# Three moves in the written-out order of a one-core hybrid mixer kernel: the gated output, the projection pieces, and one weight split

## The reference, cut to what matters

```python
h = rms_norm(x, g_pre) * (1 + scale) + shift
(sg_u, sg_v, sg_gate, dq, dk, dv, d_gate, nq, nk, nv, n_gate, f_gate, merge) = split(h @ w_in)
y_sg   = u * (W_s @ rms_norm(v) + b)                                  # spatial gating
y_diff = rms_norm((softmax(q1 k1) - lam * softmax(q2 k2)) @ v, subln) # differential attention, 4 heads
y_na   = neighbourhood_attention(nq, nk, nv, context, bias)           # 8 heads
y_f    = real(fft2(h))                                                # Fourier mixing
mixed  = sum_b sigmoid(merge_b) * ((y_b * silu(gate_b)) @ p_b)        # four branches
x      = x + gate * rms_norm(mixed @ w_out, g_post)
```

## Time and profile before

| | |
|---|---|
| Median of 3 runs | 1981.79 us (1981.74 to 1983.77) |
| The profiled execution, its own time | 1982.85 us |
| Its span in the profile | 1980.9 us |
| TensorE matmul busy | 1903.0 us, 96% of the span |
| VectorE busy | 960.9 us, 49% |
| ScalarE busy | 678.3 us, 34% |
| GpSimd busy | 593.8 us, 30% |
| Mean granted TensorE clock | 0.989 |

### The profile page before, as it was taken

One profiled execution on the slowest core, in us unless ns is written; L12 is line 12 of the kernel. 1 busy time (PEld: TensorE's weight loads), 2 busy tenths in 40 slices (PEclk: granted clock), 3 DMA queues, 4 the chain that ended last, 5 costly groups with the idle time before them and its releaser, 6 DMA issues.

```text
span 1980.9 us, 31159 instructions
## 1 busy us (share of the span) xinstructions
PE 1903.0 (96%) x12512; PEld 1762.9 (89%) x12512; DVE 960.9 (49%) x1536; ACT 678.3 (34%) x1293; POOL 593.8 (30%) x278
## 2 busy tenths in 40 slices
PE   6799999999999999999999999999999999999997
PEld 3697888989999999999878988988999999999996
DVE  5799788634355462421352144666244546433123
ACT  4322355424433221321352234453334332222221
POOL 2434322222222332233334332222322223323331
PEclk8999999999999999999999999999999999999999
DMA  8444421121111211122332221111212112212231
GB/s 305 145 164 140 164 97 43 54 83 67 65 65 65 94 66 54 65 75 75 128 117 75 91 75 65 49 49 43 96 65 75 54 65 95 75 35 83 75 126 55
DMA packets 50958, 172.16 MB, mean 87 GB/s; under 512 B 6656, under 2 KB 7296, under 8 KB 50816
## 3 DMA queue, kind: packets, MB, share of 16 engines
q1 hardware_dynamic: 41024, 146.60, 21.3%
q10 hardware_dynamic: 9792, 23.58, 3.3%
HBM read 162.82 MB, written 7.34 MB: 86 GB/s over the span
## 4 chain that ended last, share of the span: by engine, by line
PE 80%; DVE 12%; issue 3%; ACT 3%; DMA 1%; POOL 0%; SPq 0%; ACTq 0%; DVEq 0%; POOLq 0%
PE ps L1661 56%; PE ps L1549 4%; PE ps L1551 4%; PE ps L1550 4%; DVE mixed L1089 3%; PE ps L1768 2%; PE ps L1777 1%; PE ps L1787 1%; PE ps L1727 1%; PE ps L1742 1%; DMA stage<-in_w_mod 1%; DVE nparts L1313 1%; ACT Pm L998 1%; DVE Pm L1375 1%; PE ps L1812 1%
## 5 line engine op out<-in xcount | busy, mean ns | idle before, releaser
L733 POOL TENSOR_TENSOR wlo<-raw,whi 128x1024 fp32r<-128x1024 f32 x224 | 563.4, 2515 | 1233.0 <-ACT whi L791 1230.6
L1661 PE MATMUL ps<-bufB,whi 128*128 128x320 f32 x2816 | 539.4, 314 | 7.1 <-DVE vn L1215 3.9
L1661 PE MATMUL ps<-bufA,whi 128*128 128x320 f32 x2816 | 537.3, 313 | 5.3 <-DVE z L1495 1.4
L1661 PEld LDWEIGHTS ps<-bufB,whi 128*128 128x128 f32 x2816 | 441.4, 189 | 16.9 <-issue 12.3
L1661 PEld LDWEIGHTS ps<-bufA,whi 128*128 128x128 f32 x2816 | 439.3, 188 | 15.0 <-issue 10.4
L1661 PE MATMUL ps<-bufB,wlo 128*128 128x320 f32 x1408 | 322.0, 310 | 0.0
L1661 PE MATMUL ps<-bufA,wlo 128*128 128x320 f32 x1408 | 321.4, 309 | 0.0
L791 ACT ACTIVATE whi<-raw 128x1024 fp32r<-128x1024 f32 x224 | 237.5, 1060 | 212.3 <-PE ps L1661 123.6
L1661 PEld LDWEIGHTS ps<-bufB,wlo 128*128 128x128 f32 x1408 | 236.3, 189 | 0.0
L1661 PEld LDWEIGHTS ps<-bufA,wlo 128*128 128x128 f32 x1408 | 235.7, 188 | 0.0
L1495 DVE SCALAR_TENSOR_TENSOR z<-gate_m,ps 128x640 f32<-128x640 f32 x48 | 39.4, 821 | 226.2 <-PE ps L1661 225.6
(11 more groups left out here) (230 smaller groups left out, 2043.1 us busy)
## 6 DMA issues: line engine op xcount, KB each, us to landing
raw<-in_wstream SPq DMA_DIRECT2D x224, 512.0 KB, 3.2
stage<-in_wstream SPq DMA_DIRECT2D x32, 512.0 KB, 4.2
stage<-in_w_mod SPq DMA_DIRECT2D x16, 512.0 KB, 15.2
out_y_sample<-X ACTq DMA_DIRECT2D x8, 512.0 KB, 2.7
Pm<-in_rpb ACTq DMA_DIRECT2D x12, 256.0 KB, 2.9
X<-in_x_sample SPq DMA_DIRECT2D x4, 512.0 KB, 10.9
xres<-in_x_sample ACTq DMA_DIRECT2D x4, 512.0 KB, 5.1
xres<-out_y_sample ACTq DMA_DIRECT2D x4, 512.0 KB, 5.2
```

The lines of the kernel that those rows point to most:

```text
L733: pool.tensor_tensor(wlo[:, s % SPLITS, :], raw[:, s % RAWS, :], whi[:, s % SPLITS, :].bitcast(F32), ALU.subtract).then_inc(sems["lo"], 1)
L1661: ins = pe.matmul(ps[:, 2 * b + n, 0:HALF], wt[:, cols], src[:, part, base + k, n * HALF:(n + 1) * HALF], start=k == 0 and wt is hi and pa ...
```

## The change

Three moves in the order; no operation is added, removed or resized.

1. In `differential()`, `YT` of a finished head stood at the end of the segment of the next head's t = 4 unit, behind its `CB` and in front of the next scores (units 9, 14 and 19). It now stands right behind the scores step `S` of that unit. The last head's `YT` stays.
2. `interleave` gets more places. In `differential()` one before the first scores, and one before each of `TP` and `PV` of the last unit: 46 places for 64 pieces in place of 43. In `neighbourhood()` one before the first unit: 43 places for 103 pieces in place of 42.
3. In `Plan.__init__`, the one slot of layer 1 that would be split at the step `T sgv 3, 0` is split at the last `VN` instead, so behind the squares of all five tiles.

```diff
@@ def differential():
-    out, late, norm = [], [], []
+    out, norm = [None], []
     for u, (f, hh, t) in enumerate(units):
         out += [("S", "diff", u, f, hh, t, 0)] + norm + [None]
         norm = []
@@
-        out += [("CB", "diff", u, f, hh, t)] + late
-        late = []
-        if f and t < 3:
-            norm = [("NR", "diff", f - 1, t)]
-        if f and t == 3:
-            late = [("YT", "diff", f - 1)]
+        out.append(("CB", "diff", u, f, hh, t))
+        if f and t < 4:
+            norm = [("NR", "diff", f - 1, t) if t < 3 else ("YT", "diff", f - 1)]
     u = len(units) - 1
-    out += [("TP", "diff", u, *units[u]), ("PV", "diff", u, *units[u])] + late
+    out += [None, ("TP", "diff", u, *units[u]), None, ("PV", "diff", u, *units[u])]
@@ def neighbourhood():
-    out, late = [], []
+    out, late = [None], []
@@ class Plan: def __init__(self):
             if self.layer[self.first_of_slot[n]] and self.steps[self.first_of_slot[n]] == ("T", "sgv", 3, 0):
                 floor = self.at[1, ("T", "sgv", 0, 2)]
+            if self.layer[self.first_of_slot[n]] and i == self.at[1, ("T", "sgv", 3, 0)]:
+                i = self.at[1, ("VN", TILES - 1)]
             self.issue.setdefault(max(i, floor), []).append(n)
```

## The result

| | before | after |
|---|---|---|
| Median of 5 runs each | 1982.1 us (1981.74 to 1983.77) | 1991.71 us (1988.4 to 1993.44) |
| The profiled execution, its own time | 1982.85 us | 1990.2 us |
| Its span | 1980.9 us | 1988.3 us |
| Mean granted TensorE clock | 0.989 | 0.988 |

The ratio is 1.0045, with a 95% interval of 1.0035 to 1.0056: slower by 9.6 us in the medians and by 7.4 in the two profiled executions, where 1964 and a gain were forecast.

A forecast was written before the change was run, and what follows sets the result against it. TensorE, 96% busy, was taken as the bound: its work plus idle gaps and low-clock stretches. The terms summed to -17.9 us, from the profiled 1982.85 to 1964.95, or 1964 us as a median; eight-in-ten range 1956 to 1974.

The forecast's parts named there:

- Where the gates' ends fall: Differential attention: moving gates' tanh and multiply saves 3.6 us, a new wait at unit 3's transposes costs 3.5; net -0.1.
- the last unit: End of differential attention: pieces fill the gaps around transposes and `PV`, a new wait precedes the last `YT`; -8.4 us, both layers.
- neighbourhood attention: Two pieces cover the 0.5 us keys' wait before the first scores, -1.0; +1.0 allowed for pieces dealt anew; sum 0.0.
- what `YT` stands ahead of: Layer 0 around units 7 and 9, VectorE full: `YT` ahead of transposes and combination makes TensorE wait 4.4 for 2.7; +1.7 us.
- one piece ahead elsewhere: Other transposes with one piece ahead: one GpSimd subtraction per layer lengthens a VectorE operation and shows as a wait; +2.6 us.
- the price of a piece: Twelve matmuls take 1.76 us and two pieces about 3.7, so one piece covers 1.85 us of waiting.
- The squares: Layer 1: splitting last cuts TensorE's 3.85 us idle to about 0.25 and removes the half clock, -3.6 and -2.9; together -6.5 us.
- Rival (a): Squares don't gain: something else holds `VN`, the gap stays above 2.5 us and the clock falls; 1969 us, chance 0.08.
- A piece before the first scores: Differential attention, both layers: a piece fills the 0.9 us wait for VectorE's last copy of V; -1.8 us.
- Scores behind a short unit: Differential attention: waits for L998 at units 6 and 11 vanish, unit 16's falls to about 0.55; -5.4 us over both layers.
- Rival (d): Slower: GpSimd's subtractions block VectorE at most of the 24 transposes with one piece ahead; 1992 us, chance 0.05.
- Rival (b): Last unit's gap moves to `YT 3`: a longer GpSimd hold makes the 1.1 into 3 and drops the clock; 1971 us, chance 0.12.

The follow-up runs named there:

- the place in neighbourhood attention with the gates' pieces later: Kernel before with only the extra neighbourhood-attention place, and the first pieces of `F ngate 0` and `F ngate 1` one place later: 1985.92 us, ratio 1.002.
- the later split: Changed kernel with the weight split at the first piece of `F dgate 3` issued one piece later, pieces unmoved: 1981.55 us, ratio 1.0001 to the kernel before.
- the last three single edits: Squares' and `YT`'s moves plus one edit each: `YT` behind the pieces ahead, 1978.53 us; piece before first scores, 1964.24; last unit's pieces moved, 1968.65.
- best version: Squares' and `YT`'s moves, the head piece, and a piece before the last transposes taken from ahead in unit 19: 1961.67 us, ratio 0.9892 to the kernel before.
- head piece: Kernel with squares' and `YT`'s moves, plus one piece before the first differential scores, taken from ahead in unit 3: 1964.24 us, ratio 0.9911 to the kernel before.

## Why the prediction was wrong

The sum was missed by 25 us in the profiles, and five terms carry it. With both layers together, waits and clock read from the rows of before and after, "Where the gates' ends fall" was put at -0.1 and came to about +8; the last unit at -8.4 and came to about 0; neighbourhood attention at 0.0 and came to +6.4; what `YT` stands ahead of at +1.7 and came to about +6; one piece ahead elsewhere at +2.6 and came to +3.7. The other terms came out near their figures. (Read this way the terms overlap by some 1.5 us, where TensorE waits at the low clock.)

**What bounds the kernel, the price of a piece:** right, as far as it went, but for "the other stages have almost no wait": before, TensorE waits 3.36 us at 1020.52 for VectorE at the start of layer 1, and idles 29 us in the 181 before the first query transposes. No move touches these. What was missing is said below: a wait has two prices, its length and whether the clock falls behind it.

**The squares, -6.5:** right. -6.7 from the last `H` transposes to the first query transposes, -6.5 in the medians of that part alone; no wait for `vn`, the clock at 1.00. Rival (a) fell. Of the 6.5, 2.9 were clock, and that size is partly luck: with the squares as before, the wait of 3.8 to 3.9 us cost 3.4 us of clock in the profiles of three kernels (before, the places alone, and the place in neighbourhood attention with the gates' pieces later) and 1.7 in those of two (`YT` alone, and the place in neighbourhood attention alone).

**A piece before the first scores, -1.8:** right. From the first query transposes to the first scores the changed kernel takes 0.8 us longer in each layer with one piece of 1.85 more, so 1.05 less, 2.1 in both layers.

**Where the gates' ends fall, -0.1:** the step that failed first. The old waits went but for 0.3 in layer 0, and a new one did come where it was put, but at 3.8 us and not 1.5, and with the clock down. The forecast priced the gate there (1.7, by the later split) and left GpSimd to a separate term, one hit per layer, worth 1.3, at a random place. The trace has three per layer on the way to transposes, at units 3, 5 and 18. At unit 3 there was no slack, so the hit of 2.1 us counted in full, and the clock behind it (1.7 a layer) was priced nowhere. Here it isn't random: what delays VectorE, the end of a projection, is the neighbour in the list of what starts GpSimd, the beginning of the next. The rule of the Trainium skill that the prediction named (SBUF — State Buffer, "Who interferes with whom") has the trace on its side: an add of 128x2 took 2.24 us under a subtraction and 0.16 without.

**Scores behind a short unit, -5.4:** the waits went nearly as forecast, -4.6: unit 12 has a new one of 0.4 in each layer. But `YT`'s move alone takes most of them, which the text didn't separate.

**What YT now stands ahead of, +1.7 in layer 0:** right in kind. `YT 0` waits 2.4 us for VectorE's scaling, and the clock is low until 324, 1.4 + 2.0 us lost from 316 on. The walk through the queues had 1.1 before the context's scores of unit 7 (2.0 came), 1.8 before the transposes in unit 9 and 1.5 before its `PV` (none came), and none for `YT` itself; and it priced no clock.

**One piece ahead elsewhere, +2.6:** the waits at units 5 and 18, 1.0 and 0.8 in each layer, are 3.7 in all. The size of a hit was right (2.15 forecast; 2.2 and 1.6 here), and so was the slack of 0.8 at unit 18; at unit 5, where 2.6 stood, it was 1.2. The number of hits was wrong, two per layer here beside the one at unit 3. Rival (d) asked for them at most of the 24 transposes; they came at 6. That its time, 1992, is the measured one is chance. (Its "18 of the 24 have 2.6 us of slack" should read 16: of the twelve in a layer, eight have two pieces behind in the unit before.)

**The last unit, -8.4:** wrong. No wait at its transposes or `PV`, and 1.5 and 0.2 in front of and behind the last `YT`, where 1.1 and 0.2 were forecast: that much held. But "the buffers differ" looked at one pair of projections only. `YT 2` takes one buffer, so in the new order `M 0 6` and `M 0 7` both have the other, and they now meet in one place: 2.2 us for the tanh that stands behind `YT 2`'s copy and the exponentials, and the clock falls behind it in layer 1.

```profile
1365.12 0.74 ACT L797 ACTIVATE bufA<-z 128x640 fp32r<-128x640 f32 x1 [5.41 <-DVE z L1418]
...
1367.53 0.70 ACT L1032 ACTIVATE gate_m<-ps 128x640 f32<-128x640 f32 x1
1368.37 1.28 PE L1660 MATMUL ps<-bufB,whi 128*128 128x320 f32 x4 [2.17 <-ACT gate_m L1032]
```

The kernel with the places alone bears this out: its `YT 2` stands later, so `M 0 6` and `M 0 7` have different buffers, and there is no wait between them and no fall of the clock in the last unit. It takes both moves together to make this wait. Rival (b) had the 1.1 grow to 3 by GpSimd; it stayed at 1.5, and was not the cause.

**Neighbourhood attention, 0.0:** wrong, +6.4 in the stages and +6.5 by the part alone. The -1.0 wasn't there because the piece needs the buffer that is being copied; the +1.0 for the new deal had no reading behind it, and the new deal puts a projection's begin right behind `VT`.

**What would show it.** Of the signs named, the waits for `vn`, of the first scores and of `PV` for L1019 went, the one at unit 4 and the one before the last `YT` came (3.8 and 1.4 to 1.5, for 1.5 and 1), and layer 0 waits longer around unit 9. Of the signs of being wrong one came: the mean clock didn't rise from 0.989, it went to 0.988.

**The bounds and the chances.** Each part's bounds held only for itself. The forecast gave 0.05 to slower, by one mechanism that had to be everywhere. It was enough that pieces moved at all: the deal changed in 13 of 20 units and in most of neighbourhood attention, and each projection has a begin, which wants a buffer and starts a split, and an end, which wants ScalarE and VectorE. The ones that cost most: the split behind `F dgate 2`, `M 0 7` behind `M 0 6`, and the begins behind `VT`. The falls of the clock added about 6.8 us in differential attention.

What stays open: 1.3 us of layer 1's neighbourhood attention; the exact size of the split's test; and when a wait brings a fall of the clock and how long that lasts. The last is part of the spread between runs of one kernel, 5 us for the changed one: of the 15 runs of the kernel before that ran beside the last three single edits, the slowest, 1984.44 us, has the lowest mean clock, 0.986, and the fastest, 1979.85, the highest, 0.991.

## What to carry to other kernels

Filling a wait with a piece of other work moves every piece behind it. List for both orders where each projection begins (whose buffer it takes, by what stands before it in the list, and which split it starts) and ends (what it puts in front of ScalarE and VectorE) before counting the wait that is covered; here the one piece that was worth it, about -4 us, left all pieces from unit 4 on where they were. Measure the parts alone: of four, two gained 14 us together and two lost 15. And price a wait twice, for its length and for the clock behind it, the second as a range: `YT 0`'s 2.4 us brought 1.7 or 3.4 us, the 2.2 us in the last unit nothing or 1.7.

## What the runs showed of the hardware

What the clock took in an attention stage, summed over its windows, was 1.7 us before in each layer; 6.9 and 3.4 in the changed kernel; 5.2 and 0 with `YT` alone; 1.7 and 0 in the best version. How much a wait brings isn't set by its length:

| wait of TensorE | us | clock behind it, us |
|---|---|---|
| unit 3's transposes | 3.8 | 1.7 in all four places (changed kernel and places alone, both layers) |
| for `vn`, squares | 3.8 to 3.9 | 3.4 in three kernels, 1.7 in two |
| `YT 0`, layer 0 | 2.4 | 3.4 in four kernels, 1.7 in three (split later, head piece, best version) |
| for `gate_m`, last unit of the changed kernel | 2.2 | 0 in layer 0, 1.7 in layer 1 |
| unit 3's transposes, split later | 1.7 | 0 in both layers |
| last unit before, 0.8 and 1.7 within 2 us | 2.5 | 1.7 in both layers; with the place in neighbourhood attention alone, 1.7 and 5.1 |
| last unit, `YT` alone, 1.4 and 0.4 | 1.8 | 1.7 in layer 0, 0 in layer 1 |

The smallest VectorE operations lost as much time to GpSimd as a large one. Under a GpSimd subtraction of 128x1024, an add of 128x2 took 2.24 us for 0.16, an operation of 128x1 took 2.40 for 0.22, and each ended with the subtraction; a combination of 128x640 took 3.04 for 0.89.
